# An eighth 2 MB expert tile fetched before the routing flag, a fifth context room, and a compressed-key projection without doubled columns

## The reference, cut to what matters

```python
def first_block(x, positions, ...):           # h: 256 x 1024
    u = rms_norm(h, g_mix)
    h = h + hybrid_mixer(u, positions, ...)   # sparse attention (compressed, selected, window) + gated linear attention
    v = rms_norm(h, g_ffn)
    h = h + hier_moe(v, w_grp, ..., w_gate, w_up, w_down)   # 32 experts, top 2, hidden 512
    return rms_norm(h, g_final)

def compress_blocks(t, pos_emb, w1, b1, w2, b2):   # t: the compressed keys or values, 2 groups x 64
    chunks = t.reshape(bsz, g, seq // CMP_STRIDE, CMP_STRIDE, dh)
    blocks = jnp.concatenate([chunks[:, :, m:m + n_cmp] for m in range(CMP_RATIO)], axis=3)
    blocks = blocks + pos_emb
    flat = blocks.reshape(bsz, g, n_cmp, CMP_BLOCK * dh)
    return jax.nn.gelu(flat @ w1 + b1) @ w2 + b2
```

## Time and profile before

| | |
|---|---|
| three runs, median (lowest to highest) | 1176.54 us (1175.92 to 1177.77) |
| the profiled execution's own time | 1176.58 us |
| its span in the profile | 1174.7 us |
| mean granted clock of TensorE in it | 0.992 |
| TensorE, VectorE, ScalarE, GpSimd busy | 92%, 40%, 35%, 17% |
| read from HBM | 331.32 MB, 283 GB/s over the span |

### The profile page before, as it was taken

How to read it: one execution, slowest core, us unless ns; L and a number is a source line. 1 busy time by engine, 2 the same in 40 slices (tenths; PEclk the granted TensorE clock), 3 DMA queues, 4 the chain that set the end, 5 groups by cost and what they waited for, 6 DMA issues and landing times. The chain is left out here.

```text
span 1174.7 us, 17461 instructions
## 1 busy us (share of the span) xinstructions
PE 1082.5 (92%) x6884; PEld 708.3 (60%) x6884; DVE 474.4 (40%) x1046; ACT 414.9 (35%) x792; POOL 194.9 (17%) x272
## 2 busy tenths in 40 slices
PE   8999888999988979798988899998999999999997
PEld 7887545557522424344544235356887886999775
DVE  4566456445300001123433012106776545454655
ACT  5445443343110101014332002004445654444873
POOL 2002553000000000003120000004431233001550
PEclk9999999999999999999999999999999999999999
DMA  9856598556699999999999999996521414655300
GB/s 362 314 166 251 213 353 310 231 221 279 236 426 431 429 430 425 430 431 430 429 430 427 425 428 428 428 410 205 168 73 55 158 47 129 216 185 187 103 19 36
DMA packets 55721, 333.59 MB, mean 284 GB/s; under 512 B 5840, under 2 KB 6096, under 8 KB 43216
## 3 DMA queue, kind: packets, MB, share of 16 engines
q1 hardware_dynamic: 55632, 332.39, 72.1%
HBM read 331.32 MB, written 1.05 MB: 283 GB/s over the span
## 5 line engine op out<-in xcount | busy, mean ns | idle before, releaser
L490 ACT ACTIVATE ab<-w 128x1024 fp32r<-128x1024 f32 (+2 forms) x117 | 122.0, 1049 | 181.5 <-PE ps L506 174.5
L500 DVE TENSOR_TENSOR ab<-w,ab 128x1024 fp32r<-128x1024 f32 (+2 forms) x101 | 124.0, 1233 | 127.5 <-ACT ab L490 127.3
L2583 PE MATMUL ps<-w,vT 128*32 128x512 f32 x1024 | 123.4, 606 | 34.2 <-DMA w<-in_w_gate 25.1
L506 PE MATMUL ps<-ab,uA 128*128 128x512 f32 x320 | 101.3, 398 | 3.1 <-ACT gr L1597 1.3
L2583 PEld LDWEIGHTS ps<-w,vT 128*32 128x32 f32 x1024 | 28.7, 110 | 112.9 <-issue 75.3
L506 PE MATMUL ps<-UA,ab 128*128 128x256 f32 x512 | 94.4, 285 | 1.3 <-DVE ab L500 1.3
L506 PE MATMUL ps<-ab,UA 128*128 128x512 f32 (+1 forms) x288 | 87.9, 386 | 0.0
L506 PEld LDWEIGHTS ps<-UA,ab 128*128 128x128 f32 x512 | 80.3, 192 | 2.0 <-DVE ab L500 1.5
L506 PE MATMUL ps<-UB,ab 128*128 128x256 f32 x256 | 72.4, 283 | 0.0
L2633 PE MATMUL ps<-w,bT 128*32 128x512 f32 x512 | 61.7, 606 | 11.2 <-DMA w<-in_w_down 5.7
L506 PEld LDWEIGHTS ps<-ab,uA 128*128 128x128 f32 x320 | 59.8, 190 | 17.7 <-issue 3.9
(11 more groups left out here) (554 smaller groups left out, 1865.2 us busy)
## 6 DMA issues: line engine op xcount, KB each, us to landing
w<-in_w_up SPq DMA_DIRECT2D x32, 2048.0 KB, 18.6
w<-in_w_gate SPq DMA_DIRECT2D x32, 2048.0 KB, 17.4
w<-in_w_down SPq DMA_DIRECT2D x32, 2048.0 KB, 18.3
w<-in_w_ada SPq DMA_DIRECT2D x48, 512.0 KB, 7.9
w<-in_w_c SPq DMA_DIRECT2D x42, 512.0 KB, 4.4
w<-in_w_m SPq DMA_DIRECT2D x16, 512.0 KB, 4.6
w<-in_ab_out_w SPq DMA_DIRECT2D x10, 512.0 KB, 6.7
w<-in_w_out SPq DMA_DIRECT2D x8, 512.0 KB, 12.0
```

The lines of the kernel that those rows point to most:

```text
L490: e.activation(sp.a(j), w.v, ACT.Copy).then_inc(sp.whole, 1)
L500: e.tensor_tensor(sp.b(j), w.v, sp.a(j).bitcast(F32), ALU.subtract).then_inc(sp.parts[j % NAB], 1)
L506: ins = e.matmul(out_, l[x], r[y], start=start and n == 0, stop=stop and n == 2)
L2583: ins = e.matmul(t.ps[o, :], ve[:, p % 2, 2 * c + k, o], w.v[:, 2 * a + k, :], start=c + k == 0, stop=c + k == 4)
```

## The change

It has three parts.

1. **An eighth 2 MB tile ahead.** A room 33 is added that serves once. It is made of two halves of 1 MB: `grow` (128x2048) and four of the eight slices of `bSPT`, into which the three buffers bS, bP and bT are merged. Its tile is U0.3, with two transfers that count on one semaphore; TensorE picks the half (`rows_at`). The list of the first rooms grows by it, so D0.0 is the first tile behind the flag and takes room 14, and all later tiles move on by one room.
2. **A fifth context room, once.** `growc` takes the first of the context tiles behind the flag (kva.0). Two semaphores are merged into another to make room for the two new ones.
3. **kvc with each column one time.** The host's weight has 256 columns in place of 512: two tiles, two banks, 48 matmuls in place of 96. VectorE makes the doubled rows itself: per bank one evacuation of 128 partitions and two of 64 that change the half, then the eight small adds.

With two tiles and two banks less, the first stage's rooms and banks rotate by two behind kvc.

```diff
@@ Weights.take
+        if isinstance(self.views[i], tuple):
+            self.n[i] += 32
...
+            self.tiles[key] = Tile(v, (src[:, 0:x, :], src[:, x:2 * x, :]), self.sems[i], self.n[i], i)
@@ build
-        bS = sb("bS", [128, 2, 512])
-        bP = sb("bP", [128, 3, 512])
-        bT = sb("bT", [128, 3, 512])
+        bSPT = sb("bSPT", [128, 8, 512])
+        bS, bP, bT = bSPT[:, 0:2, :], bSPT[:, 2:5, :], bSPT[:, 5:8, :]
...
+        extra.append((grow[:, :, :].rearrange("p i n -> p (i n)"), bSPT[:, 3:7, :].rearrange("p i n -> p (i n)")))
+        extra.append(growc)
@@ pe_first
-            pe_linT(e, S1, "kvc", uA, uB)
+            two = [bank.take(ALL, "kvc") for _ in range(2)]
+            for c in range(2):
...
+                for m, t in enumerate(two):
...
+                    for k in range(4):
+                        o, n = slice(m * 128, m * 128 + 128), 4 * c + k
+                        ins = three(e, t.ps[:, 0:256], (a[:, k, o], b[:, k, o]), (uA[:, n, :], uB[:, n, :]), n == 0, n == 7)
@@ VectorE, kvc
-            for j, t in enumerate(bank["kvc"]):
+            for m, t in enumerate(bank["kvc"]):
...
-                e.tensor_tensor(bS[:, 0, 0:256], t.ps[:, 0:256], rsrow[:, :], ALU.mult).then_inc(t.evac, 1)
+                e.tensor_tensor(bS[:, 0, 0:256], t.ps[:, 0:256], rsrow[:, :], ALU.mult)
+                e.tensor_tensor(bS[64:128, 1, 0:256], t.ps[0:64, 0:256], rsrow[0:64, :], ALU.mult)
+                e.tensor_tensor(bS[0:64, 1, 0:256], t.ps[64:128, 0:256], rsrow[64:128, :], ALU.mult).then_inc(t.evac, 1)
@@ fetch
-            e.dma_start(w.v, w.src).then_inc(w.full, 16)
+            if isinstance(w.v, tuple):
+                for v, src in zip(w.v, w.src):
+                    e.dma_start(v, src).then_inc(w.full, 16)
+            else:
+                e.dma_start(w.v, w.src).then_inc(w.full, 16)
@@ TensorE's program
-            W.ring, W.context = Ring(*range(12)), Ring(*CONTEXT)
+            W.ring, W.context = Ring(*range(12)), Fours(CONTEXT, (*CONTEXT, GROW))
-            W.fours = Fours(FOURS, (*FOURS, 17, 18, 16))
+            W.fours = Fours(FOURS, (*FOURS, 17, 18, 16, TWO_HALVES))
@@ the host's weight
-        "w_kvc": tiles(w_in, 8, *[half(col[m], g) for m in (1, 2) for g in (0, 0, 1, 1)]),
+        "w_kvc": tiles(w_in, 8, *[half(col[m], g) for m in (1, 2) for g in range(2)]),
```

More of the change, by code:

```diff
@@ L136, in turns, with rows_at @@
                 yield
+def rows_at(v, n):
+    if isinstance(v, tuple):
+        x = v[0].shape[1]
+        return v[n // x][:, n % x, :]
+    return v[:, n, :]
 def shaped(v, shape):
@@ L163, in take @@
         key, src, i = (self.side, name), self.source[name.split("/")[-1]], ring.next()
-        self.n[i] += 16
-        self.tiles[key] = Tile(shaped(self.views[i], src.shape), src, self.sems[i], self.n[i], i)
+        if isinstance(self.views[i], tuple):
+            self.n[i] += 32
+            x = src.shape[1] // 2
+            v = tuple(shaped(y, (src.shape[0], x, src.shape[2])) for y in self.views[i])
+            self.tiles[key] = Tile(v, (src[:, 0:x, :], src[:, x:2 * x, :]), self.sems[i], self.n[i], i)
+        else:
+            self.n[i] += 16
+            self.tiles[key] = Tile(shaped(self.views[i], src.shape), src, self.sems[i], self.n[i], i)
         self.order.append(key)
@@ L391, in square @@
                 quarters(f"{name}{c}", w[:, :, 512 * c:512 * c + 512])
-        for n in ("gqk", "gv", "q", "kv", "kvc", "gr", "cq", "kva", "qa", "za", "zb"):
+        for n in ("gqk", "gv", "q", "kv", "gr", "cq", "kva", "qa", "za", "zb"):
             quarters(n, d["w_" + n])
@@ L403, in build @@
         for c in range(4):
+            if c < 2:
+                source[f"kvc.{c}"] = d["w_kvc"][:, 4 * c:4 * c + 4, :]
             source[f"w1k.{c}"] = d["w1k"][:, 4 * c:4 * c + 4, :]
@@ L441, in build @@
         over[EXTRA_FOUR] = EXTRA
-        W = Weights([x[:, :] for x in ring + ring[2:8] + extra], w_full + w_full[13:19] + [sem(f"w{x}") for x in (*EXTRA, EXTRA_FOUR)], source, over)
+        extra.append((grow[:, :, :].rearrange("p i n -> p (i n)"), bSPT[:, 3:7, :].rearrange("p i n -> p (i n)")))
+        extra.append(growc)
+        W = Weights([x if isinstance(x, tuple) else x[:, :] for x in ring + ring[2:8] + extra], w_full + w_full[13:19] + [sem(f"w{x}") for x in (*EXTRA, EXTRA_FOUR, TWO_HALVES, GROW)], source, over)
         W.ring = Ring(*range(10), *EXTRA)
@@ L1407, in build @@
         load_x, load0, load1, warm = (sem(n) for n in ("load_x", "load0", "load1", "warm"))
-        scT_zero = sem("scT_zero")
         cleared = sem("cleared")
+        SCT_ZERO, YN_ZERO, KCT_HALF, KCT_ZERO, ONES_MADE, AM_ZERO = range(1, 7)
         roped, pos_used = sem("roped"), sem("pos_used")
@@ L1463, in pe_first @@
             pe_lin(e, S1, "kv", uA, uB, 512, range(2))
-            pe_linT(e, S1, "kvc", uA, uB)
+            two = [bank.take(ALL, "kvc") for _ in range(2)]
+            for c in range(2):
+                j = S1.add(f"kvc.{c}")
+                a, b = S1.a(j), S1.b(j)
+                S1.ready(e, j)
+                for m, t in enumerate(two):
+                    if c == 0:
+                        free(e, t)
+                    for k in range(4):
+                        o, n = slice(m * 128, m * 128 + 128), 4 * c + k
+                        ins = three(e, t.ps[:, 0:256], (a[:, k, o], b[:, k, o]), (uA[:, n, :], uB[:, n, :]), n == 0, n == 7)
+                    if c == 1:
+                        ins.then_inc(t.full, 1)
+                if c == 0:
+                    S1.gone(j, ins)
+                else:
+                    S1.done[j] = (t.full, t.n)
             pe_lin(e, S1, "gr", uA, uB, 512, range(2))
@@ L1648, in act_first @@
             act_lin(e, S1, "kv", [kv[:, i, :] for i in range(2)], scaled=True)
-            act_lin(e, S1, "kvc", [])
+            act_splits(e, S1, "kvc.1", 3)
             act_lin(e, S1, "gr", [gr[:, i, :] for i in range(2)], ACT.Silu, scaled=True)
@@ L1857, in dve_first @@
             t = bank["kcrT"][0]
-            e.wait_ge(cleared, 3)
+            e.wait_ge(cleared, KCT_ZERO)
             e.wait_ge(t.full, t.n)
@@ L2582, in up @@
                             o = slice(CAP * a, CAP * a + CAP)
-                            ins = e.matmul(t.ps[o, :], ve[:, p % 2, 2 * c + k, o], w.v[:, 2 * a + k, :], start=c + k == 0, stop=c + k == 4)
+                            ins = e.matmul(t.ps[o, :], ve[:, p % 2, 2 * c + k, o], rows_at(w.v, 2 * a + k), start=c + k == 0, stop=c + k == 4)
                     if c < 3:
@@ L3405, in fetch @@
                 e.wait_ge(*use("ogT"))
-            elif w.slot in CONTEXT and W.fresh[k]:
+            elif w.slot in (*CONTEXT, GROW) and W.fresh[k]:
                 e.wait_ge(*W.done["", "pgla1.1"])
```

49 lines of the change are left out of this document (25 added, 24 removed).

## The result

| | before | changed |
|---|---|---|
| median of five runs each (lowest to highest) | 1176.54 us (1175.26 to 1177.77) | 1168.48 us (1167.95 to 1172.26) |
| ratio, 95% interval | | 0.9935 [0.9918, 0.9952] |
| the profiled execution: own time, span | 1176.58, 1174.7 us | 1167.95, 1166.1 us |

The kernel is faster, by 8.1 us at the median where 11.9 were forecast.

A forecast was written before the change was run, and what follows sets the result against it. The weight stream was taken to bound the expert stage, TensorE's own sequence the rest. The eighth tile's -4.93 and kvc's -6.95 gave -11.9 us on 1176.58: forecast 1164.6, range 1161.8 to 1168.6.

The forecast's parts named there:

- The eighth tile: Expert stage: U0.3 moved before the flag fills the DMA rest and shortens the full weight stream by 4.93 us.
- a tile worth nothing: Expert stage: rival in which TensorE is the bound and the eighth tile gains nothing, 1169.6 us; chance 0.07.
- nearly all: Expert stage: TensorE's idle 34.2 and 11.2 us were read as nearly all ended by a weight DMA.
- kvc's stretch: Compressed keys' projection and what follows to m10.2: 48 of 96 matmuls go, -5.76 us; with the other terms -6.95.
- the gap before m00: Before m00: the 1.34 us wait for ACT's evacuation of gr goes; a wait for VectorE's split adds 0.65.
- the clock's fall: In m00: granted clock of 0.87 right behind the gap; -1.70 us if it does not fall, taken as likelier than not.
- the wait before the last quarter: Before m00.3: ACT's two decay activations hold up its copy, costing +0.7 us, bounds 0 and 1.2.
- GpSimd's 0.5 us: At m10.2: GpSimd's splits gain less than TensorE, so the margin of 1.36 is short by 0.5 us, bounds 0 and 1.0.
- From m10.2 to the flag the whole program moves by that.: Between m10.2 and the routing flag: everything comes earlier by the full 6.95 us.
- is bound by TensorE's own sequence: Ahead of 296 us and behind 795 us: TensorE's sequence sets the time and has few gaps.
- One wait inside is new: Before the flag: room 32 is freed one tile's use later, by an out-projection split; the queue has 4 us to spare.
- Rival A: Around m00: the clock falls again or VectorE's chain is longer; kvc's shortening gives 5.2 us, total 1166.4; chance 0.22.

The follow-up runs named there:

- e2: The kernel before with the eighth tile and fifth context room only, kvc as before with 512 columns: 0.9967, 1172.73 us.
- e9: The changed kernel itself, run and profiled again: 0.9941, 1168.42 us.
- e4: The changed kernel with U0.1's transfer issued behind the out-projection's eight weight tiles instead of before them: 0.9924, 1167.47 us.
- e3: The changed kernel with the out-projection's banks put back by two, as in the kernel before: 0.9931, 1168.33 us.
- e1: The changed kernel without the eighth tile and the fifth context room, only kvc with each column one time: 0.9994, 1176.76 us.
- e5: The changed kernel with U0.1's transfer behind the out-projection's weights and the out-projection's banks put back: 0.9918, 1167.38 us.
- e6: The changed kernel with the bank rotation taken back from gr on, so m00 shares a bank with gr again: 0.9940, 1170.72 us.
- e11: The changed kernel with U0.1's transfer late, the out-projection's banks put back and four idle matmuls ending the expert stage: 0.9890, 1164.25 us.
- e12: The changed kernel with U0.1's transfer late and four idle matmuls ending the expert stage, the out-projection's banks as changed: 0.9912, 1167.68 us.

## Why the prediction was wrong

- **The eighth tile** was right: 4.93 us forecast, 5.1 measured over sixteen profiles (5.9 between the first two). The worst case of its rivals, a tile worth nothing, is out by e2. One reading was off without harm: "nearly all" of the 45 us in the earlier trace rows were called waits for weights, but 5.5 of them were ended by ScalarE, in both kernels.
- **kvc's stretch** was right in its mechanism: 5.8 us of matmuls for 5.76, the gap before m00 replaced by 0.69 us, the clock's fall gone, the wait before the last quarter 0.58. Up to 110 us the sum is 7.1 for a forecast of 6.95, and that it is so close is partly luck: m00 took 0.3 us more than was put (11.4 beside its wait, where gr's 11.00 had been taken for it), and GpSimd's 0.5 us did not come.
- **The step that failed** is "From m10.2 to the flag the whole program moves by that." It took the 190 us between as rigid, as did the sentence that everything ahead of 296 us "is bound by TensorE's own sequence". The chain of waits inside was not followed, and it hung on a DMA: ScalarE stood 4.95 us for the out-projection's first tile before, and TensorE behind it 0.41. A wait that already ends on a transfer gains only what the transfer gains. The burst moved 7.06 us, its fifth tile 5.5. In the changed kernel's first profile that cost 2.1 us of waiting and 1.4 of slower transposes, in its second (e9) 1.1 and nothing. e4, which lets that tile come earlier, has neither; together with the next point it is why 3.1 us reached the experts in place of 6.95.
- **A wait was overlooked.** "One wait inside is new" counted the rooms; the rotation of the banks was followed only to m00. At the router's transposes it put the first bank on the one that had just been filled: 0.87 us of waiting, 1.0 at the experts; e3 took the wait away.
- **Rival A's condition was put at the wrong place.** It priced a fall of the clock in m00, which did not happen in any of the twelve profiles without the old gap. Falls did happen at three later places (the norm's transposes, behind the router's, the end of the experts), of 0.75 to 3.4 us each, in some profiles and not in others, of one program too.
- **Not settled:** why the router's stretch falls in e1, e3, e5, e6, e11 and e12 and not in the other ten profiles; it was not tried to take the short matmuls there away. Why the burst's fourth tile is late, beyond its going together with the packet. And what the falls inside the expert stage cost, of which every profile has two to four; its length there, 483.5 to 484.5 us with the tile, shows none of them.

## What to carry to other kernels

Before calling a stretch rigid, list in it every wait that ends on a DMA or on a bank, with its margin, on all engines; an earlier start reaches the end only through those with margin left. When a change removes tiles, follow each ring that rotates (rooms, banks, split buffers) to its end, not only to the next user. A term of under 2 us is hard to tell in a kernel whose clock falls now and then and costs as much: profile a kernel twice, and read the terms from landmarks in the timelines rather than from the times.

## What was not expected of the hardware

- A 16 KB packet of the program itself, in a queue of its own, in the first 2 MB tile of a full burst: with it the tile lands in 8.7 to 9.2 us, without it in 7.8 to 8.2. Removing 96 instructions from TensorE's program went together with its coming there, and 96 waits put in elsewhere moved it off (one profile).
- TensorE's granted clock went to its lower level behind waits of 0.9 to 3.0 us, but also with no wait, behind 16 transposes and 32 matmuls of 36 columns (e5), and the same program did so at different places in its two profiles (238 us in one, 790 in the other). The Trainium skill ("TensorE: Matmul & The Clock Gate", section "What's actually happening") says that the activity is looked at on a beat that doesn't start with the kernel, so that the same kernel can differ from run to run; that the two profiles differ agrees with it.
